# Walking the columns of the rounded matmuls backwards in pieces of eight, and moving their stationary tiles by 128 bytes, in a two-layer encoder kernel

## The chip, the cores and the metric

One core of a Trainium2 chip runs the whole program. The metric is the device time of one execution in microseconds (us); the runs of a kernel are summed up by their median. TensorE (PE) multiplies, VectorE (DVE) and ScalarE (ACT) do the elementwise work, GpSimd (POOL) little, and SyncE (SP) starts the transfers of the weights.

## The reference

Two layers over 256 tokens of 1024 numbers, everything in float32:

```
for l in range(2):
    h = rms_norm(x, g_mix[l]);  qkv of four head groups = h @ w_in[l]
    four kinds of attention (stick-breaking, sliding window, chunked, forgetting), each group normed
    x = x + concat(groups) @ w_out[l]
    h2 = rms_norm(x, g_ffn[l])
    x = x + (silu(h2 @ w_gate) * (h2 @ w_up)) @ w_down                   # layer 0: 2816 hidden units
    x = x + sum over the top 2 of 8 experts of gate_e * the same form    # layer 1: 3584 hidden units each
```

## The kernel before

A float32 matmul streams its moving columns slowly. So the large products are split. A weight w is rounded to the type `float32r` as `hi`, the rest `w - hi` is rounded as `lo`, the activations are split in the same way, and a product is `xh@hi + xh@lo + xl@hi`: three rounded matmuls of 128x128 stationary numbers (activations) by 512 moving columns (weights), all into one bank of PSUM. ACT makes the `hi` halves of the weights (L1381, a copy of 128x1024) and DVE the `lo` halves (L1921, a subtraction of 128x1024), in quarters of a 128x4096 unit.

The rounded matmuls stand in five helpers: `project` (L686 to L688: projections of the groups A, B and C of each layer), `gate_up` (L942 to L944: gate and up of the dense layer), `down` (L966 to L968: down products of both layers), `half_up` (L1088 to L1090: gate and up of the experts) and `last_down` (L1105 to L1107). All other matmuls and all transposes take plain float32 operands: L690 and L814 are projections, L951 transposes the hidden rows, L786 to L788 multiply by the values.

The stationary operands of the rounded matmuls are the tiles `hT_rounded` and `qkT_rounded` (gate and up, each 8 KB per partition), and `vbuf_rounded` and `stage_rounded` (down, 4 KB each). They share their memory with the plain tiles of the same names. In `project` they are halves of weight units. The moving operands are the units `unit_0_rounded` to `unit_8_rounded` (16 KB each), the memory's first tiles; then come `x` and `xs` (8 KB each), then the four stationary tiles, each starting at a multiple of 512 bytes behind the units. A rounded matmul reads 512 bytes per partition as its stationary block and 2048 bytes as its moving row (1024 in the second dense step, whose row has 256 columns). All stationary blocks start at a multiple of 512 bytes and all moving rows of 512 columns at a multiple of 2048 from the units' start. The small tiles `ssq` and `rq0` (64 bytes each) stand far behind, among the statistics.

The work runs in this order: layer 0's attention, six dense steps, layer 1's attention with the router, and then 56 steps of the experts (8 experts, 7 steps of 512 hidden units each). A step has 24 rounded matmuls for gate, 24 for up, 24 for the down product of the step before, and 4 transposes. PE's order is written out by hand (`slots_path`). The weights are double buffered: SP loads a set of step m when the products of step m-2 are done, a 2048 KB transfer each for gate, up and down; ACT rounds them, DVE makes the rest, and PE waits on `lo_ready` for each two blocks of rows.

Of the kernel before, what the change touches and what calls it, by code (L numbers as in the profile page):

```python
# [15 lines left out]
P = 128  # L16
# [3 lines left out]
KD = D // P  # L20
# [49 lines left out]

FT = 512
QUARTERS = 4


FILLS = [
# [74 lines left out]
def trunk(nc, x_in, g_mix, w_in, b_f, g_q, g_k, swa_sinks, rel_bias, g_out, w_out, g_ffn,  # L150
          w_ff_gate, w_ff_up, w_ff_down, w_router, w_exp_gate, w_exp_up, w_exp_down, consts, out):
    with ExitStack() as ctx:
        def sb(name, shape, dt=F32):
            return ctx.enter_context(nc.sbuf_tensor(name, shape, dt))
# [17 lines left out]
        low_win = [{}, {}]  # L172
# [6 lines left out]
        units_r = [sb(f"unit_{u}_rounded", [P, UNIT], F32R) for u in range(9)]  # L179
        x = sb("x", [P, NT, D])  # L180
        xs = sb("xs", [P, NT, D])
        hT, hT_r = sb_both("hT", [P, KD, T])
        qkT, qkT_r = sb_both("qkT", [P, 2, 4, T])
        vbuf, vbuf_r = sb_both("vbuf", [P, 2, NT, GW])
# [20 lines left out]
        ssx = sb("ssx", [P, NT])  # L205
        rx0 = sb("rx0", [P, NT])
        rx = sb("rx", [P, 2 * L, NT])
        ssq = sb("ssq", [P, 2, 8])
        rq0 = sb("rq0", [P, 2, 8])
        rq = sb("rq", [P, 2, 8])  # L210
        sso = sb("sso", [P, NT])
        ro0 = sb("ro0", [P, NT])
# [189 lines left out]
        def pbank(m):  # L402
            return ps[:, m % 2, :]
# [230 lines left out]
        def _(pe):  # L634
            ident = con[:, C_ID:C_ID + P]
            up = con[:, C_UP:C_UP + 257]
            neglow = con[:, C_NEGLOW:C_NEGLOW + 256]

            def open_fill(l, name):

                n = FILL[name]
                if n >= 2:
                    pe.wait_ge(tr_free[n % 2], l * (NFILL // 2) + n // 2)
# [18 lines left out]
            def project(l, g, u, halves=(0, 1)):  # L662
                c0, cols, t = UNITS[g][u]
                m = PUNIT[g, u]
                if 0 in halves:
                    if m < NT:
                        emptied(pe, l, ("x", 2 * m))
                    if m >= 2:
                        pe.wait_ge(pr_free[m % 2], l * (NPF // 2) + m // 2)
                    if u == 0:  # L670
                        pe.wait_ge(s_win[g], 16 * (l + 1))
                    if u == 2 and g == "D":
                        pe.wait_ge(s_wd[1], 16 * (l + 1))
                    if g in SPLIT and u < 2:
                        pe.wait_ge(hx_low, NT * l + t + 1)
                for half in halves:
                    if half and m < NT:
                        emptied(pe, l, ("x", 2 * m + 1))
                    if half and u == 0 and g == "D":
                        pe.wait_ge(s_wd[0], 16 * (l + 1))  # L680
                    for k in range(4 * half, 4 * half + 4):
                        if g in SPLIT and u < 2:
                            if k % 2 == 0:
                                pe.wait_ge(w_low, NQ * l + 4 * SPLIT.index(g) + k // 2 + 1)
                            xh, xl = [part[l][:, k, t * P:(t + 1) * P] for part in (xs_high, xs_low)]
                            pe.matmul(pbank(m)[:, 0:cols], xh, high_win[g][:, k, :], start=(k == 0), stop=False)  # L686
                            pe.matmul(pbank(m)[:, 0:cols], xh, low_win[l][g][:, k, 0:cols], start=False, stop=False)
                            mm = pe.matmul(pbank(m)[:, 0:cols], xl, high_win[g][:, k, :], start=False, stop=(k == KD - 1))  # L688
# [241 lines left out]
            def gate_up(l, i, step, bufs, src, t, cols, count, kinds=(0, 1)):  # L930


                for kind in kinds:
                    full = (g_full, u_full)[kind]
                    hi, lo = weight(HIGH[l][kind], kind, cols), weight(SETS[l][i][kind], kind, cols)
                    o = ps[:, 2 * bufs + kind, 0:cols]
                    for k in range(KD):
                        if t == 0 and k % 2 == 0:

                            pe.wait_ge(lo_ready[kind], step * QUARTERS + (k // 2 + 1))  # L940
                        xhk, xlk = src[0][:, k, t * P:(t + 1) * P], src[1][:, k, t * P:(t + 1) * P]
                        pe.matmul(o, xhk, hi[:, k, :], start=(k == 0), stop=False)  # L942
                        pe.matmul(o, xhk, lo[:, k, :], start=False, stop=False)  # L943
                        mm = pe.matmul(o, xlk, hi[:, k, :], start=False, stop=(k == KD - 1))  # L944
                    mm.then_inc(full, count)

            def transposes(bufs, cols, done, count):
# [6 lines left out]
            def down(l, i, step, bufs, t, cols, done, count, first=False, part_of=None):  # L954

                hi, lo = weight(HIGH[l][2], 2, cols), weight(SETS[l][i][2], 2, cols)
                pe.wait_ge(hl_ready, done)
                blocks = cols // P
                for b in part_of or range(blocks):
                    hhb, hlb = [a[:, bufs, b * P:(b + 1) * P] for a in (hh_r, hl_r)]  # L960
                    for half in range(2):
                        part = b * QUARTERS // blocks + (half if blocks < QUARTERS else 0)
                        if t == 0 and (half == 0 or blocks < QUARTERS):
                            pe.wait_ge(lo_ready[2], step * QUARTERS + (part + 1))
                        o, c = ps[:, YB[t] + half, :], slice(half * 512, (half + 1) * 512)
                        pe.matmul(o, hhb, hi[:, b, c], start=(first and b == 0), stop=False, skip_group_check=True)  # L966
                        pe.matmul(o, hhb, lo[:, b, c], start=False, stop=False, skip_group_check=True)  # L967
                        mm = pe.matmul(o, hlb, hi[:, b, c], start=False, stop=(b == blocks - 1), skip_group_check=True)  # L968
                if not part_of or blocks - 1 in part_of:
                    mm.then_inc(d_full, count)  # L970

# [103 lines left out]
            def half_up(m, kind):  # L1075

                e, s = divmod(m, EXPERT_STEPS)
                hi, lo = weight(HIGH[1][kind], kind, FT), weight(SETS[1][m % 2][kind], kind, FT)
                o = ps[:, 2 * (m % 2) + kind, :]
                if kind == 0 and s == 0 and e:  # L1080
                    pe.wait_ge(gx_dve, e * KD + KD)
                for k in range(KD):
                    if kind == 0 and m == 0:
                        pe.wait_ge(gx_dve, k + 1)
                    if k % 2 == 0:
                        pe.wait_ge(lo_ready[kind], (DENSE_STEPS + m) * QUARTERS + k // 2 + 1)
                    xhk, xlk = xeh_r[e % 2][:, k, :], xel_r[e % 2][:, k, :]
                    pe.matmul(o, xhk, hi[:, k, :], start=(k == 0), stop=False)  # L1088
                    pe.matmul(o, xhk, lo[:, k, :], start=False, stop=False)  # L1089
                    mm = pe.matmul(o, xlk, hi[:, k, :], start=False, stop=(k == KD - 1))  # L1090
                mm.then_inc((g_full, u_full)[kind], 2)

            def last_down():

                m = MOE_STEPS - 1
                bufs, step = m % 2, DENSE_STEPS + m
                hi, lo = weight(HIGH[1][0], 2, FT), weight(SETS[1][bufs][2], 2, FT)
                pe.wait_ge(hl_ready, step * 2 + 2)
                for half in range(2):
                    for b in range(4):  # L1100
                        if not half:
                            pe.wait_ge(lo_ready[2], step * QUARTERS + b + 1)
                        hhb, hlb = [a[:, bufs, b * P:(b + 1) * P] for a in (hh_r, hl_r)]
                        o, c = ps[:, YB[0] + half, :], slice(half * 512, (half + 1) * 512)
                        pe.matmul(o, hhb, hi[:, b, c], start=False, stop=False, skip_group_check=True)  # L1105
                        pe.matmul(o, hhb, lo[:, b, c], start=False, stop=False, skip_group_check=True)
                        mm = pe.matmul(o, hlb, hi[:, b, c], start=False, stop=(b == 3), skip_group_check=True)  # L1107
                    mm.then_inc(out_full, 1)

            def scatter():  # L1110
# [1077 lines left out]
```

## Time and profile before

| | before |
|---|---|
| median of 3 runs | 1444.5 us (1443.73 to 1445.32) |
| the profiled execution | 1445.59 us |
| its span, first to last instruction | 1443.7 us |
| PE busy | 1421.5 us, 98% of the span |
| DVE busy | 1119.5 us, 78% |
| ACT busy | 935.8 us, 65% |
| HBM read | 428.33 MB, 301 GB/s over the span |
| chain that ended last | PE 90%, DVE 4%, ACT 2% |

In a row of the profile a group is an engine, a line of the kernel, what it writes and reads, how often, and how long. Matmuls are pipelined: each is shown with its own duration from first read to last write, but the next one starts before that ends. What a stream of matmuls costs is therefore the distance between two starts, which the timeline shows. PEld is the load of the stationary operand, which overlaps the matmul before it.

### The profile page before, as it was taken

The page shows a single profiled execution, that of the slowest core. Times are in us where ns is not written, and L with a number is a line of the kernel's source. Part 1 is how long each engine was busy: PE and PEld are TensorE (multiplying, and loading weights), DVE is VectorE, ACT ScalarE, POOL GpSimd, SP SyncE. Part 2 cuts the span into 40 slices and gives each one's busy share as a digit, 9 for nine tenths or more (in the row PEclk, how much of TensorE's full clock was granted, in tenths as well). Part 3 has the DMA queues.
Part 4 walks back from the last instruction along what each step waited for, and adds up shares of the span by engine and source line. Part 5 has one row for each costly group of instructions (what it writes and reads, how often), then busy time and mean ns, then how long its engine had stood idle before and what let it go on. Part 6 is the DMA issues. An engine that isn't in the chain of part 4 may idle for free.

```text
span 1443.7 us, 16880 instructions
## 1 busy us (share of the span) xinstructions
PE 1421.5 (98%) x6622; PEld 1150.3 (80%) x6622; DVE 1119.5 (78%) x1277; ACT 935.8 (65%) x1234; POOL 82.5 (6%) x102
## 2 busy tenths in 40 slices
PE   7999999999999999999999999999999999999998
PEld 4885888886885778888888888888888888888886
DVE  3565455534566699989998998999999899898996
ACT  4544444424534588777777777777877777777773
POOL 2040000001031010000000000000000000000000
PEclk9999999999999999999999999999999999999999
DMA  9342565435142899999999999999999999999992
GB/s 354 112 143 106 205 234 196 153 136 199 59 151 82 325 394 389 379 385 391 367 379 388 369 378 392 371 373 389 374 372 385 388 364 376 394 379 362 398 377 90
DMA packets 180681, 435.26 MB, mean 301 GB/s; under 512 B 5557, under 2 KB 10357, under 8 KB 180469
## 3 DMA queue, kind: packets, MB, share of 16 engines
q1 hardware_dynamic: 177540, 423.11, 79.0%
q0 software_dynamic: 3056, 11.02, 1.9%
q8 instruction: 54, 0.88, 0.3%
q14 instruction: 31, 0.25, 0.0%
HBM read 428.33 MB, written 5.78 MB: 301 GB/s over the span
## 4 chain that ended last, share of the span: by engine, by line
PE 90%; DVE 4%; ACT 2%; POOL 1%; issue 1%; DMA 1%; SPq 0%; DVEq 0%; ACTq 0%
PE ps L1088 14%; PE ps L1090 14%; PE ps L1089 13%; PE ps L968 8%; PE ps L966 8%; PE ps L967 8%; PE ps L690 4%; PE ps L814 4%; PE ps L942 3%; PE ps L944 3%; PE ps L943 3%; DVE unit_rounded L1921 2%; PE ps L951 2%; PE ps L686 1%; PE ps L688 1%
## 5 line engine op out<-in xcount | busy, mean ns | idle before, releaser
L1921 DVE TENSOR_TENSOR unit_rounded<-wmem,unit_rounded 128x1024 fp32r<-128x1024 f32 (+1 forms) x744 | 854.1, 1210 | 77.5 <-ACT unit_rounded L1381 77.1
L1381 ACT ACTIVATE unit_rounded<-wmem 128x1024 fp32r<-128x1024 f32 (+1 forms) x744 | 719.7, 1043 | 119.8 <-PE ps L1090 59.6
L966 PE MATMUL ps<-unit_rounded,vbuf_rounded 128*128 128x512 f32 x528 | 205.7, 390 | 0.0
L968 PE MATMUL ps<-unit_rounded,stage_rounded 128*128 128x512 f32 x528 | 205.6, 389 | 0.0
L967 PE MATMUL ps<-unit_rounded,vbuf_rounded 128*128 128x512 f32 x528 | 205.4, 389 | 0.0
L1088 PE MATMUL ps<-unit_rounded,qkT_rounded 128*128 128x512 f32 x448 | 177.6, 396 | 0.8 <-DVE qkT_rounded L2084 0.8
L1088 PE MATMUL ps<-unit_rounded,hT_rounded 128*128 128x512 f32 x448 | 177.4, 396 | 0.0
L1090 PE MATMUL ps<-unit_rounded,qkT_rounded 128*128 128x512 f32 x448 | 174.8, 390 | 0.0
L1090 PE MATMUL ps<-unit_rounded,hT_rounded 128*128 128x512 f32 x448 | 174.8, 390 | 0.0
L1089 PE MATMUL ps<-unit_rounded,hT_rounded 128*128 128x512 f32 x448 | 174.5, 389 | 0.0
L1089 PE MATMUL ps<-unit_rounded,qkT_rounded 128*128 128x512 f32 x448 | 174.5, 389 | 0.0
L1396 ACT ACTIVATE vbuf_rounded<-ps 128x512 fp32r<-128x512 f32 (+1 forms) x68 | 40.1, 590 | 116.5 <-PE ps L951 116.5
L968 PEld LDWEIGHTS ps<-unit_rounded,stage_rounded 128*128 128x128 f32 x528 | 99.1, 188 | 20.7
L967 PEld LDWEIGHTS ps<-unit_rounded,vbuf_rounded 128*128 128x128 f32 x528 | 99.1, 188 | 20.4
L966 PEld LDWEIGHTS ps<-unit_rounded,vbuf_rounded 128*128 128x128 f32 x528 | 99.1, 188 | 20.4
L1090 PEld LDWEIGHTS ps<-unit_rounded,qkT_rounded 128*128 128x128 f32 x448 | 84.1, 188 | 18.1
L1090 PEld LDWEIGHTS ps<-unit_rounded,hT_rounded 128*128 128x128 f32 x448 | 84.1, 188 | 18.1
L1088 PEld LDWEIGHTS ps<-unit_rounded,qkT_rounded 128*128 128x128 f32 x448 | 84.2, 188 | 17.5 <-DVE qkT_rounded L2084 1.0
L1089 PEld LDWEIGHTS ps<-unit_rounded,hT_rounded 128*128 128x128 f32 x448 | 84.2, 188 | 16.7
L1089 PEld LDWEIGHTS ps<-unit_rounded,qkT_rounded 128*128 128x128 f32 x448 | 84.2, 188 | 16.7
L1088 PEld LDWEIGHTS ps<-unit_rounded,hT_rounded 128*128 128x128 f32 x448 | 84.2, 188 | 16.5
L690 PE MATMUL ps<-wmem,hT 128*128 128x256 f32 (+2 forms) x256 | 75.2, 444 | 5.1 <-DVE stage L1667 2.2
(239 smaller groups left out, 1526.3 us busy)
## 6 DMA issues: line engine op xcount, KB each, us to landing
wmem<-in_w_exp_gate_dram SPq DMA_DIRECT2D x56, 2048.0 KB, 9.5
wmem<-in_w_exp_up_dram SPq DMA_DIRECT2D x56, 2048.0 KB, 10.0
wmem<-in_w_exp_down_dram SPq DMA_DIRECT2D x56, 2048.0 KB, 9.9
wmem<-in_w_in_dram SPq DMA_DIRECT2D x4, 3072.0 KB, 17.4
wmem<-in_w_ff_up_dram SPq DMA_DIRECT2D x5, 2048.0 KB, 8.9
wmem<-in_w_ff_gate_dram SPq DMA_DIRECT2D x5, 2048.0 KB, 9.1
wmem<-in_w_ff_down_dram SPq DMA_DIRECT2D x5, 2048.0 KB, 7.7
wmem<-in_w_out_dram SPq DMA_DIRECT2D x4, 2048.0 KB, 7.9
```

The source lines that it names most:

```text
L690: mm = pe.matmul(pbank(m)[:, 0:cols], hT[:, k, t * P:(t + 1) * P], win(l, g)[:, k, c0:c0 + cols], start=(k == 0), stop=(k == KD - 1))
L814: mm = pe.matmul(ps[:, 2 * t + half, :], oT[:, t, k * P:(k + 1) * P], wo[:, k, half * 512:(half + 1) * 512], start=first, stop=last)
L942: pe.matmul(o, xhk, hi[:, k, :], start=(k == 0), stop=False)
L943: pe.matmul(o, xhk, lo[:, k, :], start=False, stop=False)
L966: pe.matmul(o, hhb, hi[:, b, c], start=(first and b == 0), stop=False, skip_group_check=True)
L967: pe.matmul(o, hhb, lo[:, b, c], start=False, stop=False, skip_group_check=True)
L968: mm = pe.matmul(o, hlb, hi[:, b, c], start=False, stop=(b == blocks - 1), skip_group_check=True)
L1088: pe.matmul(o, xhk, hi[:, k, :], start=(k == 0), stop=False)
L1089: pe.matmul(o, xhk, lo[:, k, :], start=False, stop=False)
L1090: mm = pe.matmul(o, xlk, hi[:, k, :], start=False, stop=(k == KD - 1))
L1381: act.activation(quarter_r(HIGH[l][0 if last else kind], q, cols), quarter(SETS[l][i][kind], q, cols), ACT.Copy).then_inc(hi_ready[kind], 1)
L1921: dve.tensor_tensor(quarter_r(u, q, cols), quarter(u, q, cols), quarter_r(HIGH[l][0 if last else kind], q, cols), ALU.subtract).then_inc(l ...
```

## The change

A helper `rounded` takes the place of `pe.matmul` at all fifteen rounded calls. It re-orders the free dimension of the moving operand and of the output alike: the row is seen as two halves of 32 pieces of 8 columns (16 pieces for a row of 256); the pieces are walked from the last to the first, and each piece number is taken first from the first half, then from the second. Every column still lands in its own place. The order within a piece stays ascending. Stationary operands are read as before.

`ssq` and `rq0` are allocated ahead of `hT`, so `hT`, `qkT`, `vbuf`, `stage` and what follows them up to `rx` start 128 bytes later. The units don't move.

```
+RUN = 8
@@ trunk
         xs = sb("xs", [P, NT, D])
+        ssq = sb("ssq", [P, 2, 8])
+        rq0 = sb("rq0", [P, 2, 8])
         hT, hT_r = sb_both("hT", [P, KD, T])
         ...
         rx = sb("rx", [P, 2 * L, NT])
-        ssq = sb("ssq", [P, 2, 8])
-        rq0 = sb("rq0", [P, 2, 8])
@@ block.tensor
+            def rounded(out, stationary, moving, start, stop, **kw):
+                def walk(a):
+                    return a.rearrange("p (h c s) -> p c h s", h=2, s=RUN)[:, ::-1]
+                return pe.matmul(walk(out), stationary, walk(moving), start=start, stop=stop, **kw)
@@ project, gate_up, down, half_up, last_down: each of the three calls alike, here half_up
-                    pe.matmul(o, xhk, hi[:, k, :], start=(k == 0), stop=False)
-                    pe.matmul(o, xhk, lo[:, k, :], start=False, stop=False)
-                    mm = pe.matmul(o, xlk, hi[:, k, :], start=False, stop=(k == KD - 1))
+                    rounded(o, xhk, hi[:, k, :], start=(k == 0), stop=False)
+                    rounded(o, xhk, lo[:, k, :], start=False, stop=False)
+                    mm = rounded(o, xlk, hi[:, k, :], start=False, stop=(k == KD - 1))
```

## Rows read from the trace of the kernel before

**Rows 1.** The page: busy time of each engine in the whole span.
```profile
PE 1421.5 (98%) x6622; PEld 1150.3 (80%) x6622; DVE 1119.5 (78%) x1277; ACT 935.8 (65%) x1234; POOL 82.5 (6%) x102
```

**Rows 2.** Busy time by stretch, in the experts' steps; then PE's clock, DMA.
```profile
core 0: us, PE busy (x) PEld busy (x) DVE busy (x) ACT busy (x) POOL busy (x), PEclk, DMA share, GB/s
...
560.00:1390.00 830.00, 830.00 (x3796) 688.11 (x3795) 761.68 (x786) 636.20 (x748) 19.81 (x17) 1.00 1.02 380
1350.00:1400.00 50.00, 50.00 (x228) 41.38 (x227) 46.44 (x45) 38.05 (x42) 3.16 (x2) 1.00 1.04 395
```

**Rows 3.** Waits from 560 to 1390 us: who for whom, total us, times, longest.
```profile
ACT unit_rounded L1381 <- PE ps L1090: 54.9, 49, 1.6
DVE unit_rounded L1921 <- ACT unit_rounded L1381: 40.7, 92, 1.1
```

**Rows 4.** Timeline of PE, an expert's gate: start us, us, instruction.
```profile
820.41 0.39 PE L1090 MATMUL ps<-unit_rounded,qkT_rounded 128*128 128x512 f32 x1
...
824.49 0.39 PE L1090 MATMUL ps<-unit_rounded,qkT_rounded 128*128 128x512 f32 x1
```

**Rows 5.** Timeline of PE, the dense step with rows of 256 columns.
```profile
175.75 0.28 PE L944 MATMUL ps<-unit_rounded,hT_rounded 128*128 128x256 f32 x1
...
178.03 0.28 PE L942 MATMUL ps<-unit_rounded,qkT_rounded 128*128 128x256 f32 x1
```

**Rows 6.** Timeline of PE, plain float32 matmuls back to back.
```profile
49.71 1.89 PE L690 MATMUL ps<-wmem,hT 128*128 128x256 f32 x8
...
134.19 7.03 PE L814 MATMUL ps<-wmem,xs 128*128 128x512 f32 x16
```

**Rows 7.** Timeline of PE: short plain matmuls that wait for their stationary loads.
```profile
73.91 0.39 PE L787 MATMUL ps<-vbuf,wmem 128*128 128x64 f32 x2
...
75.25 0.39 PE L787 MATMUL ps<-vbuf,wmem 128*128 128x64 f32 x2
```

**Rows 8.** A matmul and the load of the next one's stationary block (PEld).
```profile
818.57 0.40 PE L1088 MATMUL ps<-unit_rounded,qkT_rounded 128*128 128x512 f32 x1
...
818.57 0.19 PEld L1089 LDWEIGHTS ps<-unit_rounded,qkT_rounded 128*128 128x128 f32 x1
```

**Rows 9.** Timeline of PE, dense layer: a rounded matmul that no load follows.
```profile
194.15 0.39 PE L968 MATMUL ps<-unit_rounded,stage_rounded 128*128 128x512 f32 x1
195.19 0.44 PE L951 MATMUL ps<-con,obuf 128*128 128x128 f32 x2 [0.65 <-DVE obuf L1933]
```

**Rows 10.** Groups of PE by line and shape: count, then busy us, mean ns.
```profile
L966 PE MATMUL ps<-unit_rounded,vbuf_rounded 128*128 128x512 f32 x528 | 205.7, 390 | 0.0
...
L1088 PE MATMUL ps<-unit_rounded,qkT_rounded 128*128 128x512 f32 x448 | 177.6, 396 | 0.8 <-DVE qkT_rounded L2084 0.8
...
L942 PE MATMUL ps<-unit_rounded,qkT_rounded 128*128 128x512 f32 x160 | 63.5, 397 | 0.0
...
L686 PE MATMUL ps<-unit_rounded 128*128 128x512 f32 x96 | 38.5, 401 | 0.0
...
L942 PE MATMUL ps<-unit_rounded,qkT_rounded 128*128 128x256 f32 x32 | 9.2, 288 | 0.0
...
L1105 PE MATMUL ps<-unit_rounded,vbuf_rounded 128*128 128x512 f32 x8 | 3.1, 389 | 0.0
```

**Rows 11.** One line's matmuls, 560 to 1390 us: duration ns min/median/max.
```profile
L966 PE MATMUL ps<-unit_rounded,vbuf_rounded x389: 389/389/389, 559.7 to 1389.8; 128*128 128x512 f32 x195
```

**Rows 12.** Instructions on the rounded units alone, by engine, in the same stretch.
```profile
560.00:1390.00 830.00, 813.03 (x3518) 655.89 (x3517) 676.11 (x586) 570.16 (x586) 1.00 1.02 380
```

**Rows 13.** Timeline of SP and ACT: two gate loads, and a gate's rounding.
```profile
806.74 0.37 SPq L523 DMA_DIRECT2D wmem<-in_w_exp_gate_dram  x1
...
823.55 0.37 SPq L523 DMA_DIRECT2D wmem<-in_w_exp_gate_dram  x1
...
824.12 2.00 ACT L1381 ACTIVATE unit_rounded<-wmem 128x1024 fp32r<-128x1024 f32 x2
```

**Rows 14.** DMA issues: count, KB each, median us from issue to landing.
```profile
wmem<-in_w_exp_gate_dram SPq DMA_DIRECT2D x56, 2048.0 KB, 9.5
```

More of the change, by code:

```diff
@@ L685, in project @@
                             xh, xl = [part[l][:, k, t * P:(t + 1) * P] for part in (xs_high, xs_low)]
-                            pe.matmul(pbank(m)[:, 0:cols], xh, high_win[g][:, k, :], start=(k == 0), stop=False)
-                            pe.matmul(pbank(m)[:, 0:cols], xh, low_win[l][g][:, k, 0:cols], start=False, stop=False)
-                            mm = pe.matmul(pbank(m)[:, 0:cols], xl, high_win[g][:, k, :], start=False, stop=(k == KD - 1))
+                            rounded(pbank(m)[:, 0:cols], xh, high_win[g][:, k, :], start=(k == 0), stop=False)
+                            rounded(pbank(m)[:, 0:cols], xh, low_win[l][g][:, k, 0:cols], start=False, stop=False)
+                            mm = rounded(pbank(m)[:, 0:cols], xl, high_win[g][:, k, :], start=False, stop=(k == KD - 1))
                             continue
@@ L965, in down @@
                         o, c = ps[:, YB[t] + half, :], slice(half * 512, (half + 1) * 512)
-                        pe.matmul(o, hhb, hi[:, b, c], start=(first and b == 0), stop=False, skip_group_check=True)
-                        pe.matmul(o, hhb, lo[:, b, c], start=False, stop=False, skip_group_check=True)
-                        mm = pe.matmul(o, hlb, hi[:, b, c], start=False, stop=(b == blocks - 1), skip_group_check=True)
+                        rounded(o, hhb, hi[:, b, c], start=(first and b == 0), stop=False, skip_group_check=True)
+                        rounded(o, hhb, lo[:, b, c], start=False, stop=False, skip_group_check=True)
+                        mm = rounded(o, hlb, hi[:, b, c], start=False, stop=(b == blocks - 1), skip_group_check=True)
                 if not part_of or blocks - 1 in part_of:
@@ L1087, in half_up @@
                     xhk, xlk = xeh_r[e % 2][:, k, :], xel_r[e % 2][:, k, :]
-                    pe.matmul(o, xhk, hi[:, k, :], start=(k == 0), stop=False)
-                    pe.matmul(o, xhk, lo[:, k, :], start=False, stop=False)
-                    mm = pe.matmul(o, xlk, hi[:, k, :], start=False, stop=(k == KD - 1))
+                    rounded(o, xhk, hi[:, k, :], start=(k == 0), stop=False)
+                    rounded(o, xhk, lo[:, k, :], start=False, stop=False)
+                    mm = rounded(o, xlk, hi[:, k, :], start=False, stop=(k == KD - 1))
                 mm.then_inc((g_full, u_full)[kind], 2)
@@ L1104, in last_down @@
                         o, c = ps[:, YB[0] + half, :], slice(half * 512, (half + 1) * 512)
-                        pe.matmul(o, hhb, hi[:, b, c], start=False, stop=False, skip_group_check=True)
-                        pe.matmul(o, hhb, lo[:, b, c], start=False, stop=False, skip_group_check=True)
-                        mm = pe.matmul(o, hlb, hi[:, b, c], start=False, stop=(b == 3), skip_group_check=True)
+                        rounded(o, hhb, hi[:, b, c], start=False, stop=False, skip_group_check=True)
+                        rounded(o, hhb, lo[:, b, c], start=False, stop=False, skip_group_check=True)
+                        mm = rounded(o, hlb, hi[:, b, c], start=False, stop=(b == 3), skip_group_check=True)
                     mm.then_inc(out_full, 1)
```

## The prediction

> **What bounds the kernel now.** I read the page's busy times first: PE is busy for 98% of the span and no other compute engine over 78% [rows 1]. Then the stretches of the experts' steps, some 950 us of the 1444: from 560 to 1390 us PE is busy all the time at a granted clock of 1.00, which is 2.4 GHz; DVE for 762 of the 830 us (92%), ACT for 636 (77%), and the DMA engines' share is 1.02 at 380 GB/s, 1.04 at 395 in the densest stretches [rows 2]. So three things stand close together, and the waits tell which ends last: ACT waits for PE, DVE waits for ACT, and PE has no wait in the list worth a row [rows 3]. PE sets the pace, and what its stream costs is the distance between starts.
>
> From 820.41 to 824.49 there are 18 starts of rounded matmuls of 512 columns: 4.08 / 18 = 226.7 ns each [rows 4]. With 256 columns it is (178.03 - 175.75) / 19 = 120.0 ns [rows 5]. The difference of 106.7 ns for 256 columns is 0.417 ns a column, one column per cycle of 2.4 GHz. What is left is a fixed cost: 226.7 - 213.3 = 13.3 ns and 120.0 - 106.7 = 13.3 ns. Plain float32 matmuls take two cycles a column: 8 of 256 columns in 1.89 us, less the last one's 0.38, over 7, are 215.7 ns, and 16 of 512 columns are (7.03 - 0.59) / 15 = 429.3 ns [rows 6]. Less 213.3 and 426.7 their fixed cost is 2.4 to 2.6 ns, with a stationary load before each as well. So a rounded matmul pays about 10.9 ns more than a plain one, whatever its length. That is the only thing in the stream that this change could win.
>
> **What the change touches.** It adds no instruction, wait or transfer: the same matmuls, with the moving and output columns in another order, and stationary tiles 128 bytes on. The count: 3 x 528 in `down`, 6 x 448 in `half_up`, 3 x 160 and 3 x 32 in `gate_up`, 3 x 96 in `project`, 3 x 8 in `last_down` [rows 10], together 5160. `ssq` and `rq0` are small operands of DVE and GpSimd with the same shapes at another address; I cost that at nothing, and it moves no queue.
>
> **Where 10.9 ns could come from.** The next stationary load starts with the current matmul, both at 818.57 [rows 8]. How fast it reads: matmuls of 64 columns, too short to hide it, start every 1.34 / 12 = 0.112 us (12 of them from 73.91 to 75.25) [rows 7], so 512 bytes take about 0.11 us, 4.6 bytes per ns. The moving row is read at 2048 / 213.3 = 9.6 bytes per ns in a rounded matmul and at half that in a plain one. If the two reads meet in a bank of the memory and one must stand back, a stream at one column per cycle has nothing to spare and one at two cycles a column has; the number of meetings would go by the stationary block's 512 bytes, not by the row's length. 13.3 ns is 32 cycles, one for every 16 of the 512 bytes. That fits a cost that is the same for 256 and 512 columns and missing from plain matmuls. The walk fits it too: taking pieces from both halves, 1 KB apart, the low bits of the address move at 9.6 / 2 = 4.8 bytes per ns, the load's own pace, so that two reads in the same direction would keep a fixed distance, which the 128 bytes set. Against it: the rounded matmul that no load follows (the next thing starts 1.04 us later) is shown with 0.39 us like its neighbours [rows 9], and 389 matmuls have 389 ns at minimum, median and maximum while ACT, DVE and the DMAs work on the same units [rows 11]. But ends of matmuls are modelled in this profile, so that speaks less than starts would.
>
> For the new fixed cost I have no row of a walked matmul. Bounds: at best 0 (a gain of 13.3 ns), at worst the price of the breaks, below. I take the 2.4 ns of plain matmuls [rows 6], the nearest stream in which the loads do no harm: 5160 x 10.9 = 56.2 us off PE's stream.
>
> The Trainium skill, TensorE: Matmul & The Clock Gate, Part 2 (step 1), says the opposite of this mechanism: the moving operand and the stationary load have two independent read ports, and loading the next weights takes no bandwidth from the running matmul. By that rule the phase of the addresses is worth nothing and the kernel stays at 1444.5 us.
>
> **What of it reaches the end.** Outside the experts' steps are 5160 - 4032 = 1128 rounded matmuls (4032 is 72 x 56), 12.3 us of the sum; there the chain leaves PE at times, and I take 2 us off. In the experts' steps a step takes 823.55 - 806.74 = 16.81 us [rows 13] and would take 16.81 - 72 x 0.0109 = 16.03. DVE needs 762 us of the 830 [rows 2]; PE would need 792, so DVE comes to 96% and still fits. Its waits for ACT, 40.7 us [rows 3], are for work that in the end follows PE, so they shrink with it. I cost both at nothing; if a tenth of those waits stayed and could not be hidden it would be 4 us. DMA: in the 830 us from 560 to 1390 the rate is 380 GB/s [rows 2]; they hold 3518 rounded matmuls [rows 12], which would give back 38 us, so the rate would have to be 380 x 830 / 792 = 398 GB/s, while 395 is the most that a stretch of 50 us shows [rows 2]. That is 0.8% of some 900 us, about 7 us of delay by the end. It meets a reserve: the load issued at 806.74 lands 9.5 us later, at about 816 [rows 13, 14], and is rounded from 824.12 on, 8 us later. So most of it could be hidden, and what is late next would be ACT's rounding on a load near the end. I charge 4 us, between 0 and 7.
>
> Sum against the profiled execution: 1445.6 - 56.2 + 2 + 4 = 1395.4 us. It stands 1.1 us above the median of the runs, so the forecast is 1394.3, said as 1395 us.
>
> **The rivals.**
> A. Part of it. The 128 bytes set one distance; the 288 matmuls of `project` have stationary blocks in the units, which do not move, and the reading of 4.6 against 4.8 bytes per ns is not quite in step. If a fifth to four fifths of the cost goes, the gain is 10 to 40 us: 1405 to 1435.
> B. No change. The fixed 13.3 ns belongs to rounded operands (what speaks for it: [rows 9, 11]): 1444.5 us.
> C. Slower: the breaks cost. A row has 64 pieces. One lost cycle at each is 64 x 0.42 = 26.7 ns a matmul, 5160 x 26.7 = 138 us less what the collisions give back: 1527 to 1582. It decides from 10.9 / 64 = 0.17 ns per break, less than half a cycle. For it: no matmul here reads or writes in broken runs. Against it: a piece is 32 bytes in both memories, whole and ascending.
> D. Slower: in step but on the wrong foot. Equal pace keeps a distance, also a bad one: if the load now costs the moving read two cycles for every 16 bytes in place of one, 13.3 ns more on 5160 matmuls, 69 us: 1513.
> E. Slower: the output's broken order takes PSUM to half rate, as plain matmuls need two cycles per column: 213.3 ns x 5064 rows of 512 and 106.7 x 96 of 256 are 1.09 ms, 2535 us. It decides as soon as the output can't be written one column per cycle.
>
> The Trainium skill, PSUM — Partial Sum Buffer, Specifications, states this last one: lines of 8 bytes, and any non-contiguous access pattern slows matmuls significantly. Taken by its words it would make the change much slower; taken by its reason (two columns to a line) pieces of 8 lose nothing. No run here shows which.
>
> **Chances.** Forecast 0.38, A 0.19, B 0.20, C 0.12, D 0.06, E 0.05. Within 0.2% (2.9 us) is what a measurement of this kernel can hardly tell from no change. Faster by more is the forecast and A, 0.57; within is B, 0.20; slower is C, D and E, 0.23. The range: its low end is the whole 13.3 ns gone, 5160 x 13.3 = 69 us, of which the DMA rate lets about 60 through (380 GB/s over some 950 us take 914 us at 395, 36 less; with the reserve of 8 and 13.3 x 1128 = 15 outside, 59): 1385. Its high end takes in B and a light form of C, 0.05 ns a break: 1460. That holds 0.77 and a little of C. The faster cases alone reach from 1385 to 1436.
>
> **What the profile will show.** Right: starts of rounded matmuls of 512 columns 215 to 217 ns apart and of 256 about 109, plain ones unchanged; a step of 16.0 to 16.2 us; DVE at 96%; loads landing later than 9.5 us; GB/s near 395. A would show 218 to 224 ns, or the gain in some lines and not in `project`. B shows 226.7 again. C shows a cost that halves with 256 columns. D shows one that does not. It is wrong if PE gains and the step does not: then waits of ACT on a load, or of PE on DVE, would stand in the list.

## The result, and the profile after

The changed kernel takes 1534.1 us (1533.96 to 1535.17), the kernel before on the same chip 1444.2 us: a ratio of 1.062 (95% interval 1.0605 to 1.0639), 89.9 us slower. 1395 us was forecast, with a range from 1385 to 1460. Both were wrong, and so was the sign.

The page of the kernel after answers [rows 1]: busy times, then the shares of the chain that ended last, then the group of PE's matmuls on `qkT_rounded` (all rounded calls now have one line, L644), then the gate's loads. The number of instructions has not changed.

```profile
PE 1513.2 (99%) x6622; PEld 1160.6 (76%) x6622; DVE 1126.4 (74%) x1277; ACT 936.1 (61%) x1234; POOL 75.5 (5%) x102
...
PE 95%; DVE 2%; ACT 1%; DMA 1%; POOL 0%; issue 0%; SPq 0%; ACTq 0%; DVEq 0%
...
L644 PE MATMUL ps<-unit_rounded,qkT_rounded 128*128 128x512 f32 (+1 forms) x1728 | 455.7, 408 | 0.8 <-DVE qkT_rounded L2091 0.8
...
wmem<-in_w_exp_gate_dram SPq DMA_DIRECT2D x56, 2048.0 KB, 8.4
```

PE has 91.7 us more of busy time, DVE 6.9 and ACT 0.3. The chain, 90% on PE before, is now 95% on it. The stretch from 560 to 1390 us, as in [rows 2], and the waits in it, as in [rows 3]:

```profile
core 0: us, PE busy (x) PEld busy (x) DVE busy (x) ACT busy (x) POOL busy (x), PEclk, DMA share, GB/s
560.00:1390.00 830.00, 830.00 (x3535) 646.67 (x3534) 715.93 (x737) 592.47 (x698) 9.15 (x12) 1.00 0.98 353
...
ACT unit_rounded L1388 <- PE ps L644: 71.5, 46, 1.8
DVE unit_rounded L1928 <- ACT unit_rounded L1388: 60.8, 126, 1.5
```

From 560 to 1390 us PE is busy all the time at a granted clock of 1.00 in both kernels, so the clock has no part in it. In the same 830 us it gets through 3535 instructions where it got through 3796. Everything else has more slack than before: DVE is at 86% where it was at 92%, DMA moves 353 GB/s where it moved 380, the gate's loads land after 8.4 us where they took 9.5 [rows 14], and ACT waits longer for PE. So the place is PE's stream itself, and there the distance between starts. The timeline of PE in an expert's gate (start us, us from the first start to the last end, instruction, count), to be held against [rows 4]:

```profile
936.09 3.59 PE L644 MATMUL ps<-unit_rounded,hT_rounded 128*128 128x512 f32 x14
```

Less the last matmul's own 0.41 us, 3.18 us hold 13 distances: 245 ns each, where it was 226.7. The single starts in a group show a repeating 240, 254, 248, 242, 243 ns. The same view in the dense step with rows of 256 columns, to be held against [rows 5]:

```profile
192.64 0.29 PE L644 MATMUL ps<-unit_rounded,hT_rounded 128*128 128x256 f32 x1
...
197.96 0.29 PE L644 MATMUL ps<-unit_rounded,hT_rounded 128*128 128x256 f32 x1
```

Between these two are 42 distances, 5.32 / 42 = 126.7 ns, where it was 120.0: 6.7 ns more, against 18 for 512 columns. The mean over all 4975 distances between rounded matmuls of 512 columns that follow each other, starts of groups included, goes from 228.96 to 246.90 ns: 17.9 ns. Times all 5160 rounded matmuls that is 92.6 us (a little less in truth, since 96 of them have the shorter row), and 89.9 came out at the end. The step of an expert, by SP's issues of two gate loads (start us, us):

```profile
903.30 0.37 SPq L524 DMA_DIRECT2D wmem<-in_w_exp_gate_dram  x1
...
921.40 0.37 SPq L524 DMA_DIRECT2D wmem<-in_w_exp_gate_dram  x1
```

18.10 us, where it was 16.81 [rows 13]: 1.29 us more, which is 72 rounded matmuls by 17.9 ns. The whole loss is that a rounded matmul takes about 18 ns longer. The experiments ask which part of the change does that, and what in it.

### The profile page after: what moved, and what is told of

The parts are those of the page before. It is cut to its first block, busy times and chain, and to the rows that moved or that the text cites. A ratio compares the mean times of both kernels' runs of the same rounds, so it can differ in the third digit from the quotient of the medians.

```text
span 1532.4 us, 16880 instructions
## 1 busy us (share of the span) xinstructions
PE 1513.2 (99%) x6622; PEld 1160.6 (76%) x6622; DVE 1126.4 (74%) x1277; ACT 936.1 (61%) x1234; POOL 75.5 (5%) x102
## 4 chain that ended last, share of the span: by engine, by line
PE 95%; DVE 2%; ACT 1%; DMA 1%; POOL 0%; issue 0%; SPq 0%; ACTq 0%; DVEq 0%
PE ps L644 81%; PE ps L697 4%; PE ps L821 3%; PE ps L958 2%; DMA wmem<-in_w_ff_gate_dram 1%; DVE unit_rounded L1928 1%; DMA wmem<-in_w_in_dram 0%; PE ps L794 0%; PE ps L795 0%; PE ps L771 0%; PE ps L1072 0%; ACT unit_rounded L1388 0%; PE ps L793 0%; ACT wmem L1258 0%; PE ps L709 0%; PE ps L666 0%
## 5 line engine op out<-in xcount | busy, mean ns | idle before, releaser
L644 PE MATMUL ps<-unit_rounded,qkT_rounded 128*128 128x512 f32 (+1 forms) x1728 | 455.7, 408 | 0.8 <-DVE qkT_rounded L2091 0.8
L644 PE MATMUL ps<-unit_rounded,hT_rounded 128*128 128x512 f32 (+1 forms) x1536 | 412.1, 409 | 0.0
L644 PEld LDWEIGHTS ps<-unit_rounded,qkT_rounded 128*128 128x128 f32 x1728 | 322.3, 190 | 89.1 <-DVE qkT_rounded L2091 1.0
L644 PE MATMUL ps<-unit_rounded,vbuf_rounded 128*128 128x512 f32 x1072 | 350.7, 409 | 0.0
L644 PEld LDWEIGHTS ps<-unit_rounded,hT_rounded 128*128 128x128 f32 x1536 | 288.8, 190 | 80.1
L644 PEld LDWEIGHTS ps<-unit_rounded,vbuf_rounded 128*128 128x128 f32 x1072 | 202.8, 189 | 58.6
L644 PE MATMUL ps<-unit_rounded,stage_rounded 128*128 128x512 f32 x536 | 219.1, 409 | 0.0
L644 PEld LDWEIGHTS ps<-unit_rounded,stage_rounded 128*128 128x128 f32 x536 | 101.7, 190 | 30.0
L1945 DVE TENSOR_TENSOR stage_rounded<-ps,vbuf_rounded 128x512 fp32r<-128x512 f32 (+1 forms) x68 | 46.4, 682 | 73.2 <-ACT vbuf_rounded L1403 73.1
L697 PEld LDWEIGHTS ps<-wmem,hT 128*128 128x128 f32 x256 | 47.9, 193 | 25.8 <-issue 18.1
L644 PE MATMUL ps<-unit_rounded 128*128 128x512 f32 x192 | 66.8, 422 | 0.0
L821 PE MATMUL ps<-wmem,xs 128*128 128x512 f32 x128 | 57.9, 596 | 0.1
L644 PEld LDWEIGHTS ps<-unit_rounded 128*128 128x128 f32 x192 | 36.6, 191 | 11.1
```

The lines of the kernel that those rows point to most:

```text
L644: return pe.matmul(walk(out), stationary, walk(moving), start=start, stop=stop, **kw)
L821: mm = pe.matmul(ps[:, 2 * t + half, :], oT[:, t, k * P:(k + 1) * P], wo[:, k, half * 512:(half + 1) * 512], start=first, stop=last)
L1945: dve.tensor_tensor(hl_r[:, bufs, 0:cols], ps[:, 2 * bufs, 0:cols], hh_r[:, bufs, 0:cols], ALU.subtract).then_inc(hl_ready, count)
```

## The experiments

A plain order is the order of the kernel before. The distances below are the steady ones, the mean of the last 12 distances from start to start in a group of 24 matmuls in an expert's step. Where the seven steps of an expert differ, the text says so or gives the value that most of them have. In a row of the timeline with x14 they come out as (us - the last matmul's 0.39 to 0.41) / 13, to within 1 ns.

### The two parts of the change, each alone

```
walk_only: the changed kernel, with                move_only: the kernel before, with
-        ssq = sb("ssq", [P, 2, 8])                +        ssq = sb("ssq", [P, 2, 8])
-        rq0 = sb("rq0", [P, 2, 8])                +        rq0 = sb("rq0", [P, 2, 8])
         hT, hT_r = sb_both("hT", [P, KD, T])               hT, hT_r = sb_both("hT", [P, KD, T])
         (both back behind rx)                              (both gone from behind rx)
```

> The changed kernel with ssq and rq0 back in their old place, so that the stationary tiles start where they did before: the walk alone. Theory C (each break in the order of the columns costs a part of a cycle) expects the same as the changed kernel, 1534 us within 3, and the same 244 to 246 ns between starts. Theory D (the moving read and the stationary load keep a bad distance) expects the 128 bytes to matter: anything from 1395 to 1520 us, or more than 1550.

> The kernel before with ssq and rq0 ahead of hT: the 128 bytes alone. Theory C expects 1444 us within 3 and 226.7 ns. Theory D leaves a small effect possible with the plain order too, as the two reads pass each other at another place: 1430 to 1460 us.

Measured: walk_only 1565.0 us, ratio 1.0835 (1.0817 to 1.0853), 252.3 ns a matmul. move_only 1468.0 us, ratio 1.0164 (1.0147 to 1.0181), 232 to 233 ns. The timeline of PE in an expert's gate, walk_only first; then move_only, where a line of the kernel is a line of the trace and the row names the first and the last of 14 starts:

```profile
951.71 3.69 PE L644 MATMUL ps<-unit_rounded,hT_rounded 128*128 128x512 f32 x14
```

```profile
904.15 0.40 PE L1089 MATMUL ps<-unit_rounded,hT_rounded 128*128 128x512 f32 x1
...
907.17 0.40 PE L1090 MATMUL ps<-unit_rounded,hT_rounded 128*128 128x512 f32 x1
```

(3.69 - 0.41) / 13 = 252 ns, and (907.17 - 904.15) / 13 = 232.3 ns. Both expectations were missed: 1565.0 us lies far outside theory C's 1534 within 3 and is allowed by theory D only by its "more than 1550", and 1468.0 us is above both theories' ranges. So the walk costs 120 us, the 128 bytes 23 us, and together they cost 90 us, not 143: with the walk in place the 128 bytes take 31 us off. The addresses of the stationary tiles matter by themselves, and the sign depends on the order in which the moving operand is read.

### Which side of the walk, and which order (v1, v2)

```
+            WALKS = [...]       # by expert: (parts, piece, direction) of output and of moving, stationary columns (shortened)
+            def rounded(out, stationary, moving, start, stop, **kw):
+                (oh, orun, od), (mh, mrun, md), cols = WALKS[expert]
+                ...
+                return pe.matmul(walk(out[0:cols], oh, orun, od), stationary[:, 0:cols],
+                                 walk(moving, mh, mrun, md), start=start, stop=stop, **kw)
```

Both kernels give each expert an order of its own, the first with the stationary tiles where they were in the kernel before, the second with them 128 bytes on. In the first one's experts 4 and 5 only one of the two operands is walked, so that their output columns are permuted, and expert 7 makes half of the output rows.

> Tiles as before; another walk for the rounded matmuls of each expert: 0 plain order; 1 the whole walk; 2 reversed pieces of 8 of the undivided row; 3 both halves, forward; 4 only the moving side walked; 5 only the output walked (experts 4 and 5 put columns in wrong places); 6 the whole walk with pieces of 32; 7 plain order but only 64 of the 128 stationary columns (half of the output rows left out). Theory C expects 226.7 ns for 0, about 245 for 1 to 3, the cost of 4 and 5 to add up to that of 1, and a quarter of the 18 ns left in 6 (about 231). Theory D expects 2 and 3, which are out of step with the load, to be cheap (near 227) and 4 as dear as 1, 5 free. For 7 the reading of the fixed 13.3 ns as meetings with the stationary load expects half of it, 220 ns; a cost of the rounded form itself expects 226.7.

> Tiles moved by 128 bytes as in the changed kernel; per expert: 0 plain; 1 the whole walk; 2 reversed pieces of 8 of the undivided row; 3 both halves, forward; 4 both halves, forward, pieces of 4; 5 the whole walk with pieces of 16; 6 with pieces of 64; 7 reversed pieces of 64 of the undivided row. Theory C expects a cost that halves as the pieces double: some 263 ns in 4, 245 in 1 to 3, 236 in 5, 229 in 6 and 7. Theory D expects 5 and 6 as dear as 1, since the pace of the low address bits is the same, and 2, 3 and 7 near 227.

The timeline of v1's experts, gate: plain order, the full walk, only the moving operand walked, only the output walked.

```profile
530.89 3.33 PE L659 MATMUL ps<-unit_rounded,qkT_rounded 128*128 128x512 f32 x14
...
654.70 3.69 PE L659 MATMUL ps<-unit_rounded,hT_rounded 128*128 128x512 f32 x14
...
1035.03 3.69 PE L659 MATMUL ps<-unit_rounded,qkT_rounded 128*128 128x512 f32 x14
...
1161.46 3.34 PE L659 MATMUL ps<-unit_rounded,hT_rounded 128*128 128x512 f32 x14
```

226.7, 252.4, 252.4 and 226.7 ns: **with the tiles as before, all of the walk's cost comes from the order in which the moving operand is read, and the output's order is free.** That fits theory D, but the other orders fit neither theory. Against a price for each break: in v2, halves in pieces of 64 run at the plain order's 232 to 233 ns, and pieces of 16 and 4 took 228.3 and 250.0 ns, where theory C expected 236 and 263. Against theory D: both halves forward took 243.3 ns, where it expected about 227, and pieces of 16, which it expected as dear as the whole walk, took 228.3. Half of the stationary columns (expert 7 of v1) took 230.0 ns, where a collision with the load would have given 220. The tables below have the other values.

### Other distances between the tiles (v3, v4) and the whole kernel at 96 bytes (walk_96)

```
 v3:  + bfr ahead of hT; + mhalf ahead of qkT; + fraw ahead of vbuf     (hT at 32, qkT at 64, vbuf and stage at 96)
 v4:  + ssq, rq0, bfr ahead of hT; + mhalf; + fraw                      (160, 192, 224)
 walk_96, from the changed kernel:
-        rq0 = sb("rq0", [P, 2, 8])
+        bfr = sb("bfr", [P, L, H])
```

> Small tiles are put between the large ones, so that the stationary tiles stand off by hT 32 bytes, qkT 64, vbuf and stage 96. Gate and up read qkT in experts 0, 2, 4, 6 and hT in 1, 3, 5, 7, with these orders of the columns: plain in 0 and 1, the whole walk in 2 and 3, its form with pieces of 16 in 4 and 5, reversed pieces of 8 of the undivided row in 6, the walk with pieces of 32 in 7. The down products, at 96 bytes: plain, whole walk, pieces of 16, of 32, both halves forward by 16, whole walk by 4, reversed by 16 and by 32 undivided. Theory P (the moving read and the stationary load collide where their addresses fall together modulo 256 bytes) expects every order's cost to depend on the offset, the plain one between 216 and 245 ns, and the whole walk's somewhere under 230 at one of the offsets. Theory R (what matters is only whether a tile starts at a multiple of 512 bytes) expects 232 ns for plain order at 32, 64 and 96 alike and 245 for the whole walk.

> As v3 with hT off by 160 bytes, qkT by 192, vbuf and stage by 224. Theory P: other values than in v3, since none of these distances is the same modulo 256. Theory R: the same values as v3 in every place.

Distances in ns by the bytes that the stationary tiles stand on, from v1 to v4 (and v6 for pieces of 16 and 32 at 0):

| order of the moving row | 0 | 32 | 64 | 96 | 128 | 160 | 192 | 224 |
|---|---|---|---|---|---|---|---|---|
| plain | 226.7 | 233.3 | 233.3 | 234.0 | 232 | 233.3 | 228.8 | 233.3 |
| the change's walk (halves, 8, backwards) | 252.4 | 260.0 | 260.0 | 240.0 | 245 | 245.0 | 244.8 | 246.2 |
| halves, 16, backwards | 233.3 | 233.3 | 226.7 | 228.3 | 228.3 | 228.3 | 228.3 | 233.3 |
| halves, 32, backwards | 236.7 | 233.3 | | 240.0 | | 233.3 | | 233.3 |

Several cells have a second value in a part of their groups: the walk at 64 bytes runs at 240.0 in 3 of 14, the walk at 96 at 244.8 in 2 of 7, pieces of 16 at 160 at 233.3 in 5 of 14, pieces of 32 at 96 at 233.3 in 2 of 7. The rows of v3 behind the largest and the smallest of them, both with `qkT` at 64 bytes: the walk in pieces of 8, then of 16.

```profile
785.73 3.80 PE L667 MATMUL ps<-unit_rounded,qkT_rounded 128*128 128x512 f32 x14
...
1042.65 3.33 PE L667 MATMUL ps<-unit_rounded,qkT_rounded 128*128 128x512 f32 x14
```

One shift can cost one order 7 ns and give another 5 to 7 back. No shift brings any order under 226.7. Neither theory holds as it was put: theory P's walk under 230 ns is at none of the shifts, and theory R's equal values fail for the walk (260.0 and 240.0).

> The changed kernel with the stationary tiles 96 bytes away from where they were before, in place of 128 (ssq and bfr ahead of hT). The down products showed 240.0 ns there with the whole walk, against 244.4 at 128 and 251.8 at 0. Theory P: 4872 rounded matmuls outside the projections at 13.3 ns more than before and 288 at some 25 more, 72 us: 1516 us within 5. A theory in which something else than these distances makes the time (DMA, other engines) expects it to stay at 1534.

walk_96 took 1538.2 us (ratio 1.0638, 1.0615 to 1.066), where 1516 within 5 was expected: a miss. The same order at the same 96 bytes ran at 240.0 in five of seven steps of v3's down products, and here at 245 to 246 in nearly all groups (and at 260.0 in some), with the changed kernel's pattern of five:

```profile
939.34 3.60 PE L644 MATMUL ps<-unit_rounded,hT_rounded 128*128 128x512 f32 x14
```

So the steady distance does not follow from order and alignment alone; one order has several steady patterns, and the changed kernel itself has some groups at 240.0. What picks one isn't known.

### Is it the stationary load at all? (v5)

The table of v1, with 1 to 112 stationary columns in place of 128, so that only so many output rows are computed; tiles as before. The load's record gets shorter with it, from 0.19 us with 128 columns [rows 8] to 0.08 us with one, so a part of the load stays:

```profile
655.94 0.08 PEld L675 LDWEIGHTS ps<-unit_rounded,hT_rounded 128*1 128x1 f32 x1
```

> Tiles as before. The stationary block is cut to fewer of its 128 columns, which leaves out output rows, and so shortens the load beside the moving read. Gate, experts 0 to 7: plain with 32, plain with 8, whole walk with 32, whole walk with 8, reversed pieces of 8 undivided with 8, walk by 16 with 8, plain with 96, plain with 16. Up: plain with 64, plain with 1, whole walk with 64, whole walk with 1, reversed 8 with 1, walk by 16 with 1, plain with 112, both halves forward by 8 with 8. Down as gate, with both halves forward by 4 with 8 in expert 7. Theory P (the walk's cost is collisions of the moving read with the stationary load) expects the cost to go with the load: 213 to 220 ns at 8 columns and 1 for every order, and between that and 252 for the whole walk at 32 and 64. Theory M (the moving read alone is slowed by its broken order) expects the whole walk to stay near 240 to 252 ns with a load of 1 column. For the plain order the two readings of the fixed 13.3 ns are 216 (a collision) and 226.7 (a cost of the rounded form).

The timeline, up products: plain order with one stationary column, the full walk with one in two steps of the same expert, and with 64:

```profile
657.08 3.37 PE L675 MATMUL ps<-unit_rounded,hT_rounded 128*1 128x512 f32 x14
...
909.38 3.52 PE L675 MATMUL ps<-unit_rounded,hT_rounded 128*1 128x512 f32 x14
...
927.28 3.59 PE L675 MATMUL ps<-unit_rounded,hT_rounded 128*1 128x512 f32 x14
...
781.41 3.71 PE L675 MATMUL ps<-unit_rounded,qkT_rounded 128*64 128x512 f32 x14
```

Plain order: 228.8 ns with 1 column (231.7 in two of seven steps), 231.1 with 8, 228.9 with 16, 230.0 with 64 (from v1) and 226.7 with 128. **The fixed 13.3 ns stay when 127 of 128 columns of the load are taken away**, so the collision on which the forecast rested, one that goes by the stationary block's bytes, is not what they are. That a load instruction goes before each matmul did not change in any run. The walk: 240.0 in three steps and about 245 in four with 1 column, the same two values with 8 and 32, 253.3 with 64, 252.4 with 128. Of its 25.7 ns, 11 to 16 stay with a load of one column (240.0 or 245 - 228.8), which reads 4 bytes per partition in place of 512; the rest comes with the load's size. So theory M's range for the walk with one column holds, and theory P's 213 to 220 does not. The walk on the tiles moved by 128 bytes runs in these same two values with all 128 columns, so the move takes off about as much as the small load does; whether it is the same thing is not shown, since no run has both.

### Breaks, or addresses? (v6, v7, walk_quarters, walk_64)

```
 v6:  the table of v1 for each product of each expert, with 1 to 16 parts and pieces of 1 to 128
 v7:  plain order, tiles as before, but every moving row starts some floats further on than the one before (wrong weights are read)
+                return units_r[unit][:, at + by:at + by + FT]
 walk_quarters: walk_only with                      walk_64: walk_only with
-  "p (h c s) -> p c h s", h=2, s=RUN               -RUN = 8
+  "p (h c s) -> p c h s", h=4, s=RUN               +RUN = 64
```

> Tiles as before, 128 stationary columns, 24 other orders of the columns, one per expert and product. Gate: plain; both halves reversed by 16; forward by 16; four quarters reversed by 8, forward by 8, reversed by 16, forward by 16; undivided reversed by 16. Up: undivided reversed by 1, 2, 4, 32 and 64; both halves forward by 32, reversed by 32, forward by 64. Down: eighths forward by 8, reversed by 8, forward by 16; both halves forward by 128, reversed by 4, forward by 2; quarters forward by 4; sixteenths forward by 8. Theory P expects any order that leaves the addresses modulo 256 bytes as they were to cost 226.7 ns (pieces of 64 and 128) and the others to scatter between 216 and 262 without a rule by the number of breaks. Theory M expects a rising cost with the number of breaks: pieces of 1, 2 and 4 dearest.

> Plain order of the columns, tiles as before, 128 stationary columns. In the experts the moving row starts some numbers further than it should, in the same memory (it reads wrong weights; the output is not the reference's). The start advances by a fixed number of floats from one matmul to the next, modulo 64: gate, experts 0 to 7: 0, 2, 4, 6, 8, 12, 16, 32; up: 62, 60, 56, 48, 24, 40, 20, 1. Down, by the place in the triple of hi, lo, hi: (0, 8, 0), (0, 4, 0), (0, 16, 0), (0, 32, 0), (0, 8, 16), (0, 56, 0), (8, 8, 8), (0, 2, 0). Theory S (the memory serves an address only at its turn, a turn that comes round every 13.3 ns, so that 215.8 ns is rounded up to 226.7 because all rows start at the same address modulo 256 bytes) expects the advance to matter: 216 to 219 ns at some of them, 220 to 231 at others, 226.7 again at 0 and at (8, 8, 8). Theory F (13.3 ns is a fixed cost of the rounded form) expects 226.7 everywhere.

The timeline of v6: quarters in pieces of 8 backwards, the whole row backwards column by column, and the whole row backwards in pieces of 64.

```profile
902.97 3.41 PE L675 MATMUL ps<-unit_rounded,hT_rounded 128*128 128x512 f32 x14
...
536.52 3.43 PE L675 MATMUL ps<-unit_rounded,qkT_rounded 128*128 128x512 f32 x14
...
1030.09 3.34 PE L675 MATMUL ps<-unit_rounded,qkT_rounded 128*128 128x512 f32 x14
```

232.2, 233.3 and 226.7 ns. With the tiles as before, v1 and v6 give:

| order | neighbouring pieces apart | breaks a row | ns |
|---|---|---|---|
| plain | - | 0 | 226.7 |
| backwards by 64 | 256 bytes back | 8 | 226.7 |
| halves by 64, halves by 128 | 1 KB and multiples of 256 | 8, 4 | 226.7 |
| backwards by 1, 2, 4, 8, 16, 32 | that piece back | 512 to 16 | 233.3 |
| quarters by 8, backwards or forwards | 512 bytes | 64 | 232.2, 231.1 |
| quarters by 16, backwards; forwards | 512 bytes | 32 | 240.0; 231.2 |
| halves by 16, backwards; forwards | 1 KB | 32 | 233.3; 240.0 |
| halves by 8, backwards; forwards | 1 KB | 64 | 252.4; 243.3 |
| halves by 4, backwards; by 2, forwards | 1 KB | 128; 256 | 253.3; 333.3 |
| eighths by 8, backwards; forwards | 256 bytes | 64 | 258.8; 233.3 |

512 breaks cost 6.6 ns in one order and 64 cost 25.7 in another, so it is not a price for each break. Theory P's 226.7 for pieces of 64 and 128 came; its upper bound of 262 for the others did not (333.3), and theory M's rise with the number of breaks did not either. Orders whose pieces are whole multiples of 256 bytes cost nothing, however far they jump. In v7 an advance of 0 gives 226.7 and each of the 23 other patterns lies between 230.0 and 234.8, so both theories miss: the 216 to 219 ns of theory S is nowhere, and it is not theory F's 226.7 everywhere. One of the patterns, (8, 8, 8), is a constant 32 bytes: with the stationary tiles in their old place and the moving rows moved, it runs at 233.3 ns, as the plain order does with the stationary tiles moved by 32 bytes and the rows in place. Two whole kernels carry the two findings, no price for each break and free pieces of 256 bytes, to the end time.

> Every rounded matmul walks its columns in pieces of 8, from the last to the first, but from four quarters of the row in place of two halves; tiles as before. It has as many breaks as the changed kernel, 64 a row. A price per break expects the time of the walk alone, 1565 us, or at least that of the changed kernel, 1534. If what counts is which addresses follow one another, the 232 ns of this order in an expert's gate carry over: 5.5 ns on 5160 matmuls, 28 us: 1472 us within 4.

> The walk alone with pieces of 64 in place of 8, so that each piece is 256 bytes; tiles as before. It goes backwards and takes both halves in turn like the change. If going backwards or changing halves costs by itself, 1450 to 1565 us; if only the order of the addresses modulo 256 bytes counts, which this walk leaves as it was, 1444.5 us within 2.

walk_quarters took 1470.4 us (ratio 1.0173, 1.0156 to 1.019), walk_64 1445.1 us (1.0005, 0.9995 to 1.0014), both as expected from the addresses. Their timelines in the same gate:

```profile
901.14 3.41 PE L644 MATMUL ps<-unit_rounded,hT_rounded 128*128 128x512 f32 x14
```

```profile
886.80 3.34 PE L644 MATMUL ps<-unit_rounded,hT_rounded 128*128 128x512 f32 x14
```

232 and 227 ns. Quarters by 8 have the same 64 breaks and the same 32-byte pieces as the change's walk without the move, and cost 25 us in place of 120. The walk in pieces of 256 bytes costs nothing.

## Why the prediction was wrong, point by point

**What bounds the kernel** held. PE sets the pace, and 96 to 97% of what was added to its stream reached the end (89.9 of 92.6 us; 120.4 of 124.9 in walk_only, 23.3 of 24.3 in move_only). The step and the distance between starts moved as one, also as forecast.

**The size of the fixed cost** held, its cause did not. 13.3 ns a matmul are there [rows 4, 5], and 10.9 more than in plain matmuls. The step "13.3 ns is 32 cycles, one for every 16 of the 512 bytes" made an account out of a coincidence of numbers. With one stationary column the bytes are 1/128 and the distance is 228.8 ns, where a cost that goes by these bytes would have come to about 216. The rows that spoke against it, [rows 9, 11], were set aside because ends are modelled; they pointed the right way. The fixed cost was not taken away by any order, alignment or size of load, and what it is stays open.

**The term 5160 x 10.9 = 56.2 us** fell with it, and its sign. Two things stood in its place. The moving operand's order costs 24.2 ns in the mean over all starts with the tiles as before, and the move changes that to 17.9. Both were priced at nothing or a gain, by bounds "at best 0, at worst the price of the breaks": the upper bound was right to be there and was then not used, since the range took in only 0.05 ns a break. No row of before shows a matmul that reads in any order but the plain one, so nothing in the trace bounded this from above, and the high end should have reached rival C's 1527 to 1582.

**The move at nothing but a phase.** `ssq` and `rq0` themselves do cost nothing: DVE's busy time is 1119.5 us before and 1120.2 in move_only. But the stationary tiles behind them cost 23 us by their new address, when the moving rows are read plainly. The prediction gave the 128 bytes a part only as what sets the distance between two reads; that a place at a multiple of 512 bytes could be worth something, so that leaving it is a loss of its own, was not weighed.

The Trainium skill, TensorE: Matmul & The Clock Gate, Part 2 (step 1), with its independent read ports, agrees with v5 in that the load is not what makes the fixed 13.3 ns. It does not agree with move_only: by it the phase of the stationary tiles is worth nothing, and the runs have 1468.0 against 1444.7 us. Nor does the walk in v5 agree, which takes 253.3 ns beside a load of 64 columns and 240.0 or 245 beside one of 1 column.

**Rival C** had the right place and a number near the result (1527 to 1582, 1534.1 measured), with the wrong mechanism. A price for each break would make walk_quarters as slow as walk_only; it is 95 us faster. Its mark in the profile, a cost that halves with 256 columns, came out as 6.7 against 18 ns, a bit over a third. The shorter row also has its halves 512 bytes apart and not 1 KB, the distance at which quarters of the long row cost 5.5 ns; that fits, and was not tried apart. **Rival D**, the fixed distance on the wrong foot, is too small and needs the load that v5 takes away; but v5 also shows that the load adds to the walk's cost (240.0 or 245 with one column, 252.4 with all). That the step of the read with the load decides does not fit: pieces of 16, in the same step, run at 228.3 to 233.3 ns, and both halves forward, out of step, at 243.3. **Rival B** had the distance right, 226.7 ns, for the plain order and the orders by 64, and the fixed cost as one that the walk can't take away. **Rival A** needed a gain per matmul, which nothing showed.

**Rival E** fell: the output alone in the walk's order runs at 226.7 ns. The Trainium skill, PSUM — Partial Sum Buffer, Specifications, has any non-contiguous pattern slow a matmul significantly; for an output in pieces of 8 float32 columns the trace of v1 does not agree.

**DMA, 4 us, and attention, 2 us**, had nothing to act on. As the stream got slower, the rate fell to 353 GB/s and the loads landed sooner. The 395 GB/s behind this charge were not quite the most: the 50 us from 1335 of the kernel before show 397, which would make the charge a little smaller.

**Shown**: the walk's cost is in the order in which PE reads the moving rows (v1: moving side alone 252.4 ns, output side alone 226.7), and there is a second cost by the place of the stationary tiles (move_only, v3, v4) or of the moving rows (v7). That pieces of whole 256 bytes are free is seen in three orders of v6 and one whole kernel. **Open**: by what rule the other orders cost 4 to 107 ns, why backwards is dearer than forwards in some splits (258.8 and 233.3 in eighths), and forwards dearer in one (240.0 and 233.3 in halves by 16), whether the places of the two operands count each by itself or against each other (both moved alike was not run), and what picks among the patterns of one order (240.0 or 245 to 246 ns). A conflict of reads within 256 bytes is a guess that none of these runs settles.

Nothing measured beat the kernel before: of some 80 combinations of order, alignment and load size none had a distance under 226.7 ns, and the kernel before has exactly that.

## What to carry to other kernels

Before a fixed cost in a stream is put down to a collision, take the supposed partner away in one experiment (here one stationary column in place of 128); a match of numbers is no evidence, and an order that no row shows has no upper bound from the trace, so the range has to take in the likeliest rival on the other side whole. Keep the moving rows of rounded matmuls in ascending, unbroken order, or in pieces of whole 256 bytes where they must be broken, and keep stationary and moving tiles a whole multiple of 512 bytes apart, as in the kernel before: two small tiles of 128 bytes together, allocated in between, cost 23 us here (whether 256 bytes would do was not run). Writing the output in pieces of 8, backwards and from both halves, cost nothing.

## What the runs showed of the hardware

- A rounded matmul of 512 columns takes 226.7 ns from start to start at best. The same row read backwards column by column takes 233.3 ns, read in 8-column pieces from halves 1 KB apart 240.0 to 260.0 (252.4 with the tiles as before), in 2-column pieces forwards from the halves 333.3.
- Walking the PSUM output in pieces of 8, from the last to the first and from both halves, costs nothing (226.7 ns) where the moving rows are read plainly.
- The moving row in pieces of 64 or 128 columns (256 or 512 bytes), in another order, costs nothing (226.7 ns; the whole kernel 1445.1 against 1445.0 us).
- Stationary tiles 32 to 224 bytes past their old place cost 2 to 7 ns a matmul in the plain order (228.8 to 234.0 ns).
- A stationary load of one column in place of 128 saves nothing in the plain order (228.8 against 226.7 ns).
